# A software-pipelined pooling stage and a modulation vector moved to the merge loop, in an 8-core decoder layer

## What is computed

```
mod = (silu(c) @ w_ada + b_ada).reshape(B, 9, 1, D)          # mod 0 .. 8
x = x + 0.5 * mod[2] * swiglu(modulate(rms_norm(x), mod[0], mod[1]), ...)
h = modulate(rms_norm(x), mod[3], mod[4])
u_pool, q, k, v, ga, gb = split(h @ w_in)
y_pool = multiscale_pool(u_pool, pool_mix, pool_scale) @ w_pool_up
y_attn = swa_sink_attention(q, k, v, ...) @ w_attn_up
x = x + mod[5] * ((sigmoid(ga) * y_pool + sigmoid(gb) * y_attn) @ w_o)
x = x + 0.5 * mod[8] * swiglu(modulate(rms_norm(x), mod[6], mod[7]), ...)
```

## Time and profile before

| | |
|---|---|
| median of 2 runs | 3250.29 us (3241.21 and 3259.36) |
| the profiled execution | 3255.51 us |
| its span on the slowest core (core 3) | 3253.7 us |
| spans of the eight cores | 3192.4 to 3253.7 us |
| mean granted TensorE clock per core | 0.932 to 0.940 of full speed |

### The profile page before, as it was taken

The page is one execution under the profiler, slowest core; times in us unless marked ns, Lnnn a source line. Parts: engine busy times, 40 slices in busy tenths (PEclk is TensorE's granted clock), DMA queues, the critical chain, the costliest instruction groups (busy, mean ns, idle before and its releaser), DMA issues.

```text
span 3253.7 us, 45977 instructions; the slowest of 8 cores (3192.4 to 3253.7 us)
## 1 busy us (share of the span) xinstructions
PE 2767.4 (85%) x16166; PEld 1415.1 (43%) x16166; DVE 1760.0 (54%) x2510; ACT 431.5 (13%) x703; POOL 573.6 (18%) x515
## 2 busy tenths in 40 slices
PE   0257999999999999477578899897599999999998
PEld 0134556566666565223143344343244444444443
DVE  0131556666666667778832233346446666666666
ACT  2020000000000001333221111122200000000001
POOL 1140011011011002622311222335300000000003
PEclk9778999999999999788588899999799999999999
DMA  9979586775676576246486754776145555544442
GB/s 200 140 85 135 66 104 81 90 102 76 83 104 82 78 101 96 35 52 78 67 109 81 91 75 65 98 97 94 27 74 78 78 78 78 76 74 74 75 77 107
DMA packets 427515, 281.49 MB, mean 87 GB/s; under 512 B 15136, under 2 KB 409504, under 8 KB 427040
## 3 DMA queue, kind: packets, MB, share of 16 engines
q0 software_dynamic: 421968, 257.97, 60.7%
q1 hardware_dynamic: 5328, 20.60, 1.8%
HBM read 528.10 MB, written 8.39 MB: 165 GB/s over the span
## 4 chain that ended last, share of the span: by engine, by line
PE 72%; DMA 12%; DVE 9%; issue 3%; ACT 1%; POOL 1%; another core or an unknown queue 0%; DVEq 0%; POOLq 0%; ACTq 0%
PE ps L336 72%; DMA arena<-w_ada 4%; DMA arena<-w_attn_up 3%; DMA arena<-w_ffn_down 3%; DVE arena L710 2%; DVE arena L375 1%; DVE arena L481 1%; DMA arena<-w_ffn_gu 1%; DVE arena L403 1%; DVE arena L384 1%; POOL arena L410 1%; DMA arena<-w_o 1%; DVE arena L771 1%; DVE arena L867 0%; ACT arena L406 0%
## 5 line engine op out<-in xcount | busy, mean ns | idle before, releaser
L336 PE MATMUL ps<-arena 128*128 128x384 bf16 (+4 forms) x16166 | 2767.4, 331 | 476.3 <-DMA arena<-w_ada 128.7
L336 PEld LDWEIGHTS ps<-arena 128*128 128x128 bf16 (+1 forms) x16166 | 1415.1, 99 | 1828.1 <-issue 660.6
L481 DVE SCALAR_TENSOR_TENSOR arena<-ps,arena 128x384 f32<-128x384 f32 (+1 forms) x1710 | 1093.6, 667 | 112.2 <-PE ps L336 12.1
L456 DVE TENSOR_TENSOR arena<-arena,ps 128x384 bf16<-128x384 f32 (+1 forms) x220 | 133.6, 607 | 714.4 <-PE ps L336 708.4
L454 ACT ACTIVATE arena<-ps 128x384 f32<-128x384 f32 (+1 forms) x220 | 117.3, 534 | 1825.9 <-PE ps L336 1054.4
L281 POOL DMA_DIRECT2D arena<-w_ffn_gu x88 | 101.0, 1150 | 889.2 <-PE ps L336 889.2
L281 POOL DMA_DIRECT2D arena<-w_ffn_down x44 | 30.7, 699 | 844.8 <-PE ps L336 844.8
L867 DVE SCALAR_TENSOR_TENSOR arena<-ps,arena 128x512 f32<-128x512 f32 x176 | 125.5, 747 | 39.5 <-PE ps L336 29.4
L281 POOL DMA_DIRECT2D arena<-w_ada x72 | 83.8, 1166 | 258.5 <-PE ps L336 257.6
L375 DVE RECIPROCAL arena<-arena 128x512 f32<-128x512 f32 (+1 forms) x30 | 90.8, 3025 | 43.2 <-ACT arena L373 43.2
L863 POOL TENSOR_TENSOR arena<-arena 128x512 f32<-128x512 f32 x80 | 101.2, 1272 | 48.2 <-ACT arena L860 42.0
(11 more groups left out here) (52 smaller groups left out, 510.5 us busy)
## 6 DMA issues: line engine op xcount, KB each, us to landing
arena<-w_ffn_gu POOLq DMA_DIRECT2D x88, 1024.0 KB, 15.2
arena<-w_ada POOLq DMA_DIRECT2D x72, 1024.0 KB, 18.8
arena<-w_ffn_down POOLq DMA_DIRECT2D x44, 1024.0 KB, 11.9
arena<-w_in POOLq DMA_DIRECT2D x24, 1024.0 KB, 13.3
arena<-xT SPq DMA_DIRECT2D x16, 576.0 KB, 19.4
arena<-w_o POOLq DMA_DIRECT2D x8, 1024.0 KB, 10.6
yT<-arena SPq DMA_DIRECT2D x16, 512.0 KB, 3.8
arena<-w_pool_up POOLq DMA_DIRECT2D x8, 512.0 KB, 19.7
```

Of the source, the lines that this page charges most:

```text
L336: ins = e.matmul(out_ap, l, r, start=(i == 0), stop=(i == n - 1), **kw)
L456: S.op("dve", lambda e: e.tensor_tensor(out=act[sl_][jj][:, b0:b1], in0=sg[q][:, 0:n], in1=pu[:, 0:n], op=ALU.mult), reads=[ru, sgres[q]], ...
L481: S.op("dve", lambda e: e.scalar_tensor_tensor(out=xT[:, m, b0:b1], in0=po[:, 0:n], scalar=gate_v[gate_k][:, m:m + 1], in1=xT[:, m, b0:b1] ...
```

## The change

Three parts.

1. In the pooling stage, the 8 matmuls with the group's matrix become a function `poolmix(g)`. It is called for g-1 at the end of group g, so that the next group's products stand between DVE's chain and its reader. The last one, `poolmix(3)`, is called behind the loop. `pooled` gets a second pair of buffers and `U` a second buffer, one for each half. The tile `pu_in` is handed back right behind its last product, and `pm` behind its `poolmix`.
2. `compute_mod(7, ...)` is taken out of the pooling stage. The merge loop calls it once for every mp, between `stage_gu(mp)` and `compute_mod(8, [mp])`.
3. Vectors 7 and 8 are now built up at the same time, so vector 8 uses columns 16 to 31 of bank 7.

```diff
@@ compute_mod
+                cbase = 16 if i == 8 else 0
                 for mm in range(2):
                     ch = cb * 2 + mm
-                    mm_group(banks[7][:, ch:ch + 1],
+                    mm_group(banks[7][:, cbase + ch:cbase + ch + 1],
...
@@ mixer, pooling stage
-            U, T1, T2 = tmpA, tmpB, tmpC
+            pooledb = [pooled, [sbf3(TO), sbf3(TO)]]
+            presb = [pres, [Res(), Res()]]
+            Ubuf = [tmpA, sf323(TT)]
+            T1, T2 = tmpB, tmpC
+            def poolmix(g):
+                tpm, srm, hpm = pmt.pop(g)
+                for cc2 in range(2):
+                    for (b0, b1) in TB2:
...
+                W.done(hpm)
             for g in range(4):
                 slu_, sru_ = W.pop(("pu_in", g), ...)
+                hpu = W.last
                 slm_, srm = W.pop(("pm", g), ...)
                 for cc in range(2):
+                    U, Ur = Ubuf[cc], Ubr[cc]
+                    pl, plr = pooledb[g % 2][cc], presb[g % 2][cc]
                     for (b0, b1) in TB1:
...
-                    compute_mod(7, [2 * g + cc])
+                    if cc == 1:
+                        W.done(hpu)
...
-                for cc2 in range(2):
-                    for (b0, b1) in TB2:
...
-                W.retire()
+                if g >= 1:
+                    poolmix(g - 1)
+            poolmix(3)
...
@@ mixer, merge loop
             for mp in range(9):
                 if mp < 8:
                     stage_gu(mp)
+                    compute_mod(7, [mp])
                     compute_mod(8, [mp])
                 if mp >= 1:
                     stage_down(mp - 1)
```

More of the change, by code:

```diff
@@ L351, in compute_mod @@
                 if cb == 7:
-                    S.op("dve", lambda e, i=i: e.tensor_tensor(out=mod[:, i * 16:(i + 1) * 16], in0=banks[7][:, 0:16],
+                    S.op("dve", lambda e, i=i: e.tensor_tensor(out=mod[:, i * 16:(i + 1) * 16], in0=banks[7][:, (16 if i == 8 else 0):(32 if i == 8 else 16)],
                                                                 in1=bada[:, i * 16:(i + 1) * 16], op=ALU.add),
@@ L744, in mixer @@
             pres = [Res(), Res()]
-            U, T1, T2 = tmpA, tmpB, tmpC
-            Ur, T1r, T2r = Res(), Res(), Res()
+            sbf3, sf323 = scratch_alloc()
+            sbf3(8 * TO)
+            sbf3(8 * TO)
+            sbf3(TO)
+            sbf3(TO)
+            pooledb = [pooled, [sbf3(TO), sbf3(TO)]]
+            presb = [pres, [Res(), Res()]]
+            Ubuf = [tmpA, sf323(TT)]
+            Ubr = [Res(), Res()]
+            for _r in presb[1] + Ubr:
+                S.stamp(_r)
+            T1, T2 = tmpB, tmpC
+            T1r, T2r = Res(), Res()
+            pmt = {}
+            def poolmix(g):
+                tpm, srm, hpm = pmt.pop(g)
+                for cc2 in range(2):
+                    for (b0, b1) in TB2:
+                        pm_, rm_ = ps_next()
+                        mm_group(pm_[:, :], [(tpm[:, cc, cc2 * 128:(cc2 + 1) * 128], pooledb[g % 2][cc][:, b0 - HALO:b1 - HALO]) for cc in range(2)],
+                                 [srm, presb[g % 2][0], presb[g % 2][1]], rm_)
+                        ch = 2 * g + cc2
+                        S.op("act", lambda e, pm_=pm_, ch=ch, b0=b0, b1=b1: e.activation(
+                            out=mixedT[:, ch, b0 - HALO:b1 - HALO], in_=pm_[:, :], func=AF.Copy, scale=pscale[:, ch:ch + 1]),
+                            reads=[rm_, R["par"]], writes=[mres[ch]])
+                W.done(hpm)
             for g in range(4):
@@ L749, in mixer @@
                 slu_, sru_ = W.pop(("pu_in", g), [(v3(16, 256), kview(w_in)[:, :, g * 256:(g + 1) * 256])])
+                hpu = W.last
                 t = v3(16, 256)(slu_)
                 slm_, srm = W.pop(("pm", g), [(v3(2, 256), pmix[g].rearrange("(k p) n -> p k n", p=128))])
-                tpm = v3(2, 256)(slm_)
+                pmt[g] = (v3(2, 256)(slm_), srm, W.last)
                 for cc in range(2):
+                    U, Ur = Ubuf[cc], Ubr[cc]
+                    pl, plr = pooledb[g % 2][cc], presb[g % 2][cc]
                     for (b0, b1) in TB1:
@@ L758, in mixer @@
                                  [sru_] + hr(b0, b1), ru_)
-                        S.op("act", lambda e, pu_=pu_, n=n, b0=b0, b1=b1: e.activation(out=U[:, b0:b1], in_=pu_[:, 0:n], func=AF.Copy),
+                        S.op("act", lambda e, pu_=pu_, n=n, b0=b0, b1=b1, U=U: e.activation(out=U[:, b0:b1], in_=pu_[:, 0:n], func=AF.Copy),
                              reads=[ru_], writes=[Ur])
-                    compute_mod(7, [2 * g + cc])
-                    S.op("dve", lambda e: e.tensor_scalar(out=U[:, 0:HALO], in0=U[:, 0:HALO], scalar1=valid, scalar2=None, op0=ALU.mult),
+                    if cc == 1:
+                        W.done(hpu)
+                    S.op("dve", lambda e, U=U: e.tensor_scalar(out=U[:, 0:HALO], in0=U[:, 0:HALO], scalar1=valid, scalar2=None, op0=ALU.mult),
                          reads=[Ur, R["cpar"]], writes=[Ur])
@@ L775, in mixer @@
                         sh *= 2
[L776 to L779, removed]
+                    S.op("dve", lambda e, src=src, pl=pl, w=w, U=U: e.scalar_tensor_tensor(out=pl[:, 16:TO], in0=src[:, HALO + 16:TT],
+                                                                                            scalar=1.0 / w, in1=U[:, HALO + 16:TT],
+                                                                                            op0=ALU.mult, op1=ALU.subtract),
+                         reads=[srcr, Ur], writes=[plr])
                     dst, dstr = dsts[di % 2]
@@ L783, in mixer @@
                          reads=[srcr, R["cpar"]], writes=[dstr])
-                    S.op("dve", lambda e, dst=dst, cc=cc: e.tensor_tensor(out=pooled[cc][:, 0:16], in0=dst[:, 0:16],
-                                                                          in1=U[:, HALO:HALO + 16], op=ALU.subtract),
-                         reads=[dstr, Ur], writes=[pres[cc]])
-                for cc2 in range(2):
-                    for (b0, b1) in TB2:
[L789 to L795, removed]
-                W.retire()
+                    S.op("dve", lambda e, dst=dst, pl=pl, U=U: e.tensor_tensor(out=pl[:, 0:16], in0=dst[:, 0:16],
+                                                                               in1=U[:, HALO:HALO + 16], op=ALU.subtract),
+                         reads=[dstr, Ur], writes=[plr])
+                if g >= 1:
+                    poolmix(g - 1)
+            poolmix(3)
+            Ur = Ubr[0]
             if debug:
```

## The result

The changed kernel takes 3284.55 us (median), the kernel before, measured beside it, 3247.07 us. Ratio 1.0106, 95% interval 1.0085 to 1.0126: slower by 28 to 41 us. The profiled execution took 3273.73 us. The forecast was 3284, 33.5 us slower.

The account below looks back on a forecast made before the run. The pooling stage was taken as bound by the PE, ACT, DVE, PE handover, the merge loop by DMA waits from the four-slot ring. Gain 30.5 and cost 64 made +33.5 on 3250.3: 3284 us, range 3248 to 3312.

Parts of the forecast that it names:

- The pooling stage: Products, warm poolmix, last wait, cold poolmix and barrier were to sum to 81.5 us against 112.0, a gain of 30.5.
- DVE's lag: Pooling stage: DVE's longest chain, 7.8 us, just matches three products, so DVE keeps up; a lag of 1 is possible.
- The pau tile: Start of the merge loop: pau lands at 85 us, after stage_gu's first product; costed at nothing, upper end 3.
- Vector 7 for nothing, vector 8 at the seam: Merge loop: vector 7's w_ada tile fits the 23 us of idle DMA; vector 8's issues at the seam ahead of w_o.
- 8.0 for each seam: Merge loop: each of eight seams grows by 8.0 us, 64 in all; bounds 46 to 85.
- Both waits move by the same 8.0: Merge loop seam: w_o and pau land 8.0 us later; PE still waits 3.2 for pau; iteration 8.0 longer.
- a tile's share of the stream: Burst at the seam: landing steps on core 3 were 7.9, 8.2 and 6.8 us; a w_ada tile taken as 8.0.
- move from 8 to 6: Sign of being wrong: the steps between landings in the merge loop's burst move from 8 us to 6 or to 10.
- The price estimated by the page of the Trainium skill: Burst: 2.1 MB a tile at about 358 GB/s, 5.9 us; eight would cost 47, giving 3267 us.
- A: Rival on the merge loop: moved tiles are free in the idle DMA time, only the 30.5 gain stays, 3220 us; chance 0.12.
- B: Rival on the merge loop's burst: cheaper than core 3 shows, 5.7 us a tile, 46 in all, 3266 us; chance 0.17.
- C: Rival: burst dearer, 10.6 us a tile, 85 in all, 3305; or pooling stage gains only 21, then 3314; chance 0.17.

Follow-up runs that it names:

- e3_no_vec7: Against the changed kernel, vector 7's eight w_ada tiles and their matmuls left out, so vector 7 is not computed; 3215.12 us, ratio 0.9924 to the kernel before.
- e4_mid_gu: Against the changed kernel, vector 7's tile used in the middle of stage_gu, behind its second round, not at its end; 3225.14 us, ratio 0.9953 to the kernel before.
- e1_pipe_only: Against the changed kernel, vector 7 put back into the pipelined pooling stage, merge loop as before the change; 3252.13 us, ratio 1.0019 to the kernel before.
- e5_two_seam: Against the changed kernel, vector 8's tile loaded and used twice, so two w_ada tiles precede w_o at each seam; 3333.39 us, ratio 1.0276 to the kernel before.

## Why the prediction was right, and where it was not

The forecast difference, +33.5, lies within the 28 to 41 measured. That the median of 3284.55 stands beside a forecast of 3284 is chance: against the 3277.31 given with it the forecast is 7 us high.

**The pooling stage** came out as worked: 82.2 for 81.5, idle times 7.71 and 1.09, warm poolmix, and a gain of 31.3 on the mean core against 30.5. DVE's lag, which I had bounded by 1, was 0.1. The pau tile cost PE nothing when the loop began.

**Vector 7 for nothing, vector 8 at the seam.** The w_ada tile that fills the fourth slot is free, and the other one stands in front of w_o, as the DMA order shows. e3_no_vec7 and e4_mid_gu confirm that place and not quantity is what costs: the same eight tiles are worth 59 us with one more in front of w_o at each seam, and some 9 when they are used in the middle of stage_gu.

**8.0 for each seam** is nearly the mean (62.5 / 8 = 7.8), but the step behind it failed. It said "Both waits move by the same 8.0" and gave a tile's share of the stream as 8.0. Over the cores, pau's landing moved from 27.3 to 32.9, by 5.6, and PE's wait for it, which the prediction kept at 3.2, went from 0.6 a seam in the mean to nothing. w_o's landing moved from 8.7 to 16.0, by 7.3: w_ada as first of the burst takes 10.2 where w_o took 8.7, and w_o follows it 5.8 later (on core 5, 11.5 and 5.0: landings at 1895.8 and 1900.8).

PE spends this time in a new wait for w_ada (3.2 a seam) and a longer one for w_o (5.1 where it was 1.9). And stage_down runs slower behind the two waits: its 64 matmuls take 16.9 from the first to the last, 15.6 in before. So the seam costs 7.3 + 1.2 - 0.6 = 7.9, as the period says (68.2 - 60.4 = 7.8). On core 5 PE starts stage_down at the lower clock and needs 14.75 for 56 matmuls. Core 0 of before, which had waited 1.09, ran that stretch at a granted clock of 1.00:

```profile
1875.65 9.76 PE L336 MATMUL ps<-arena 128*128 128x512 bf16 x44 [1.09 <-DMA arena<-w_o]
1885.67 2.76 PE L336 MATMUL ps<-arena 128*128 128x512 bf16 x12 [0.26 <-DVE arena L867]
```

That is 12.8 for the same 56, so the restart is worth up to 2 us.

A share that was too high (8.0 for 5.8), a first landing and a restart that were missing, and a wait that was kept though it went: that these made nearly 8.0 is luck. One of the prediction's own signs of being wrong was steps between landings that "move from 8 to 6", and they stood at 5.5 to 5.8 in after; but the mean core had 6.2 in before already, so the 8 was a size of core 3 and not of the kernel. I had read it there, at one seam of the core with the slowest burst of all (31.5 from the first slot to pau, against 25.1 and 25.2 on cores 0 and 7). In e1_pipe_only and e3_no_vec7, which load the same tiles in this loop, no core's burst is above 28.1.

The price estimated by the page of the Trainium skill (5.9 a tile, "DMA: Bandwidth & Descriptors", section "Where 436 GB/s comes from") fits the share of the stream, 5.8 in after and 6.0 to 6.3 in e5_two_seam, better than my 8.0. As a price of the seam it falls short, since it has neither the first tile's landing nor the restart.

**The rivals.** A (free tiles) is refuted for this order and was not far from e4_mid_gu. B (5.7 a tile) was right on the stream and wrong on the sum. C's dearer burst didn't come. In the case against A, "all three steps of the burst are above 6.8" is not quite so: the third is 6.8.

What stays open: why core 3 of the profile before needed 31.5 for its burst while the others needed 25 to 29, and why the spread is small in after (31.7 to 34.6). The cores reach the burst at different times; that they collide there was not tested by itself.

## What to carry to other kernels

In a ring whose tiles are loaded strictly in the order of their use, the cost of moving a load is read at the place where the slots come free, not from the bytes or the idle share of the DMA engines: the same eight tiles cost 59 us in front of the one that PE waits for, and some 9 us in the middle of the stage before it. Look for the places in each iteration where the engines are idle and a slot can be given back, and leave each load more than its best landing time. A software pipeline that closes a compute wait also closes the time in which loads used to land: without the move it gained nothing.

## What the runs showed of the hardware that was not expected

As first tile of a burst w_o (rows of 2048 columns) landed 8.7 after its issue in the mean of before (7.7 to 11.0), a w_ada tile of the same size (256 columns from each row) 10.2 in after (8.7 to 15.3). That the shape makes the difference is likely, but no run changes the shape alone. Behind two waits of 4 to 4.5 us with 32 one-column matmuls between them, the granted clock stood at 0.50 (1.2 GHz) for the next 3.5 us; behind a wait of 1.09 it was 1.00 (2.4 GHz). And a core can be off by itself: with the shorter burst the eight merge loops took 480 to 517 in before, with core 3 as the long one, but 482 to 496 in e1_pipe_only, which has the same loop.
